# Sparse attention layer: the index keys' unit moved first, one root for both latents, index products between the query tiles

## The chip, the cores and the metric

The kernel runs on one core of a Trainium2 chip. The metric is the device time of one execution in microseconds, lower is better. A core has TensorE (PE, the matrix products; PEld is its weight load), VectorE (DVE), ScalarE (ACT), GpSimd (POOL) and SyncE (SP, which here only issues transfers). They run on their own and wait for one another through semaphores.

## The reference

The program is a decoder trunk of two layers over 512 tokens of width 1024. Each layer has a feed-forward part, a mixer, and another feed-forward part. The change is in the mixer of the second layer, a sparse attention with an index:

```python
q_lat = rmsnorm(h @ w_dq, q_norm_g)                        # 256 wide
q = (q_lat @ w_uq).reshape(bsz, s, DSA_HEADS, DSA_LATENT)  # 16 heads of 128
kv = rmsnorm(h @ w_dkv, kv_norm_g)                         # 128 wide
q_idx = (q_lat @ idx_w_q).reshape(bsz, s, IDX_HEADS, IDX_DIM)   # 16 heads of 64
k_idx = layernorm(h @ idx_w_k, idx_ln_g, idx_ln_b)         # 64 wide
w_idx = (h @ idx_w_w) * (IDX_HEADS ** -0.5 * IDX_DIM ** -0.5)
...
idx_logits = jnp.einsum('bqhd,bsd->bqhs', qib, k_idx)
score = jnp.einsum('bqhs,bqh->bqs', jax.nn.relu(idx_logits), wb)
score = jnp.where(causal, score, -jnp.inf)
_, sel = lax.top_k(score, topk)                            # the 128 best keys of a query
```

Each query then attends, with 16 heads, to its 128 selected keys alone, with a softmax and a relative-position bias.

## The kernel before

Activations lie transposed: a tile is 128 features by 512 tokens. Weights are streamed in units of 128 x 1024 numbers, in a ring of four slots. SP loads a unit into `w_raw`; ACT rounds it to `w_hi` (`produce_hi`, L471); DVE takes the rest, `w_lo` (`produce_lo`, L801); PE multiplies in three products per 128-row block (L1457 to L1459), which is why one unit of eight blocks is 24 matmuls. PE and each of the other engines follow their own instruction streams in the order in which the code was written; nothing is reordered.

The attention layer is `mix1`. Its head has four units. In the first two (`first_units`, L1476 to L1478) PE also forms the token norm: eight sums (L1549), and a spread of the root over the partitions (L1557). Units 0 and 1 give the query latent, unit 2 the key latent, unit 3 the index keys (64 rows) and index weights (16 rows). DVE scales each unit by the token norm (L1285, L1287, L1289). `latent_sums` (L1830) sums squares, `latent_rms` on DVE takes the root (some twelve tiny steps, L1274 and L813 to L818), `latent_spread` (L1836) spreads it. There are two such roots: one for the query latent, and a later one for the key latent and the index keys. The index keys are centred by a small product (L1857).

The body has 24 query tiles of six matmuls each (`q_tile`, L1881 to L1883): tiles 0 to 7 hold the index queries of two heads each, tiles 8 to 23 one head of attention queries each. ACT evicts them (L699). Then there are 48 index products r = 0 to 47 (L1902): three query blocks of 16 heads, each a product of 64 rows by 256, 384 or 512 keys. Even heads use partitions 0 to 63 of `index_q` and `index_k`, odd heads 64 to 127; the second copy of `index_k` is made by a transfer on POOL's queue (L452). ACT rectifies each product (L711), and DVE multiplies it by the head's weight and adds it up (L1343, L1346). From r = 16 on, DVE also runs the selection of the block before: MAX8 and MATCH_REPLACE8 (L1329, L1331), one round per product in block 2, one round per two products in block 3. The rings are four deep: PE's product r waits for the rectified product r - 4, and this one for DVE's sum r - 8:

```python
for r in range((TT - 1) * IH):
    ...
    if r >= 4:
        pe.wait_ge(d_relu, r - 3)
    pe.matmul(ps[:, r % 4, 0:w], ...).then_inc(d_ix, 1)
    if r % 3 == 2 and r // 3 < AH - 1:
        q_tile(KT + 1 + r // 3)
```

So before the change nine query tiles run first, and then three index products and one tile in turn. When DVE has done its last sum, the attention proper starts (L1364 on DVE, L1947 on PE).

Of the kernel before, what the change touches and what calls it, by code (L numbers as in the profile page):

```python
# [21 lines left out]
ALU = mybir.AluOpType  # L22
ACT = mybir.ActivationFunctionType
# [40 lines left out]
def build_program(nc, a, out):  # L64
    ctx = ExitStack()
    with ctx:
# [88 lines left out]
        index_k_centred = at("index_k_centred", [IDIM, TOK], 40)  # L155
# [13 lines left out]
        cmat = at("cmat", [IDIM, IDIM], 99)  # L169
# [57 lines left out]
        if "mix1" in UB:  # L227
            parts[UB["mix1"] + 3] = 3
# [48 lines left out]
        d_mul, d_hi, d_ql, d_kv, d_kn, d_dup, d_tr, d_trev = (sem("d_" + n) for n in ("mul", "hi", "ql", "kv", "index_k", "dup", "tr", "trev"))  # L277
# [5 lines left out]

        R0, X0, V_ORDER = 9, 17, (1, 2, 3, 0)
# [10 lines left out]
        def _(sp):  # L295
# [42 lines left out]
            def column_params():  # L338
# [5 lines left out]
                sp.dma_start(pcols[0:IDIM, 11:12], a["idx_ln_g"].rearrange("l h -> h l")).then_inc(cols_landed, 16)  # L344
                sp.dma_start(pcols[0:IDIM, 12:13], a["idx_ln_b"].rearrange("l h -> h l")).then_inc(cols_landed, 16)
# [57 lines left out]
        def _(pool):  # L403
# [33 lines left out]
            if "mix1" in STAGES:  # L437
# [13 lines left out]
                pool.wait_ge(d_kn, 2)  # L451
                pool.dma_start(index_k[IDIM:2 * IDIM, :], index_k[0:IDIM, :]).then_inc(d_dup, 16)  # L452
# [9 lines left out]
        def _(act):  # L462
# [77 lines left out]
            def mix0(nxt):  # L540

                n = UB["mix0"]
                act.wait_ge(cols_landed, 16 * 6)
# [130 lines left out]
            def mix1(nxt):  # L674
# [4 lines left out]
                for t in range(1, 4):  # L679

                    act.wait_ge(tile_out, 4 + T1 + t)
                    act.activation(sq[:, t - 1, :], q_latent_raw[:, t - 1, :] if t < 3 else kv_raw[:, :], ACT.Square).then_inc(d_raw, 1)
                    produce_hi(n + t + SLOTS)
# [3 lines left out]
                act.wait_ge(d_cen, 1)  # L687
# [15 lines left out]
                for t in range(KT):  # L703
                    q_out(t)
                q_out(KT)
                for r in range((TT - 1) * IH):
# [5 lines left out]
                    if r % 3 == 2 and r // 3 < AH - 1:  # L712
                        q_out(KT + 1 + r // 3)
# [1331 lines left out]
```

## Time and profile before

| | |
|---|---|
| median of three runs | 2184.98 us (2181.61 to 2185.51) |
| the profiled execution | 2183.87 us, its span 2182.1 us |
| PE busy | 2130.7 us, 98% of the span |
| PEld, DVE, ACT busy | 80%, 56%, 33% |
| POOL busy | 2% |
| mean granted TensorE clock | 0.992 |
| chain that ended last | PE 68%, DVE 8%, issue 2%, ACT 2% |
| DMA queues | q1 29.8% of the 16 engines' span |

The busy share is an average over very different stages: the feed-forward parts keep PE full, while the attention layer, about 1541 to 1770 us, has stretches in which DVE sets the pace. What a change there is worth has to be read there.

### The profile page before, as it was taken

The numbers are of one execution on the slowest core, as the hardware profiler recorded it, in microseconds if no ns is written. First come the engines' busy times: TensorE is split into PE (matmuls) and PEld (weight loads), VectorE is DVE, ScalarE is ACT, GpSimd is POOL, SyncE is SP. The second block draws the span as 40 slices with busy tenths as digits, with TensorE's granted clock in tenths as the row PEclk, the third lists the DMA queues.
The fourth block names the chain that finished last, engine by engine and source line by source line (L and its number), as shares of the span: only waits on it lengthen the run. The fifth ranks groups of instructions, "written<-read, shape, count | busy, mean of one in ns | idle before, by whom it ended". The sixth has DMA issues, their size and how long they took to land.

```text
span 2182.1 us, 27827 instructions
## 1 busy us (share of the span) xinstructions
PE 2130.7 (98%) x10065; PEld 1736.5 (80%) x10065; DVE 1225.0 (56%) x1948; ACT 729.9 (33%) x1013; POOL 51.8 (2%) x95
## 2 busy tenths in 40 slices
PE   8999999999999999999999999999997999999998
PEld 7888888788887778888888888888765678888887
DVE  6535446586658986445356544445578645435444
ACT  4222224334335542222224222223366643222223
POOL 0000000000000000000000000000002300000000
PEclk9999999999999999999999999999999999999999
DMA  6333424322243324454443333333300113333321
GB/s 171 96 99 96 110 83 105 91 65 59 68 127 90 83 69 115 106 116 106 112 105 106 102 97 96 96 96 87 87 23 1 40 49 97 96 97 96 97 84 61
DMA packets 357868, 195.14 MB, mean 89 GB/s; under 512 B 14747, under 2 KB 349734, under 8 KB 357782
## 3 DMA queue, kind: packets, MB, share of 16 engines
q1 hardware_dynamic: 355110, 184.21, 29.8%
q0 software_dynamic: 2672, 9.80, 2.8%
q8 instruction: 52, 0.85, 0.2%
q14 instruction: 34, 0.28, 0.0%
HBM read 191.07 MB, written 2.79 MB: 89 GB/s over the span
## 4 chain that ended last, share of the span: by engine, by line
PE 68%; DVE 8%; issue 2%; ACT 2%; DVEq 0%; ACTq 0%
PE ps L1457 19%; PE ps L1459 19%; PE ps L1458 19%; PE ps L1641 1%; PE ps L1947 1%; PE ps L1935 1%; DVE w_lo L801 1%; DVE index_scores L1346 1%; PE ps L1656 1%; PE ps L1657 1%; PE ps L1658 1%; PE ps L1476 1%; PE ps L1478 1%; PE ps L1477 1%; DVE index_scores L1331 1%
## 5 line engine op out<-in xcount | busy, mean ns | idle before, releaser
L471 ACT ACTIVATE w_hi<-w_raw 128x1024 fp32r<-128x1024 f32 x351 | 371.5, 1060 | 1055.1 <-PE ps L1459 974.4
L1457 PE MATMUL ps<-h_hi,w_hi 128*128 128x512 f32 x1632 | 637.6, 391 | 0.0
L1459 PE MATMUL ps<-h_hi,w_lo 128*128 128x512 f32 x1632 | 635.3, 389 | 0.0
L1458 PE MATMUL ps<-h_lo,w_hi 128*128 128x512 f32 x1632 | 635.2, 389 | 0.0
L801 DVE TENSOR_TENSOR w_lo<-w_raw,w_hi 128x1024 fp32r<-128x1024 f32 x351 | 428.8, 1222 | 288.3 <-ACT w_hi L471 288.1
L1457 PEld LDWEIGHTS ps<-h_hi,w_hi 128*128 128x128 f32 x1632 | 306.4, 188 | 65.3 <-issue 2.2
L1459 PEld LDWEIGHTS ps<-h_hi,w_lo 128*128 128x128 f32 x1632 | 306.4, 188 | 63.8
L1458 PEld LDWEIGHTS ps<-h_lo,w_hi 128*128 128x128 f32 x1632 | 306.5, 188 | 62.8
L1457 PE MATMUL ps<-act_hi,w_hi 128*128 128x512 f32 x704 | 274.1, 389 | 0.0
L1459 PE MATMUL ps<-act_hi,w_lo 128*128 128x512 f32 x704 | 274.0, 389 | 0.0
L1458 PE MATMUL ps<-act_lo,w_hi 128*128 128x512 f32 x704 | 274.0, 389 | 0.0
L907 DVE SCALAR_TENSOR_TENSOR x<-ps,x 128x512 f32 (+1 forms) x112 | 77.4, 691 | 276.2 <-PE ps L1459 275.2
L929 DVE TENSOR_TENSOR prod<-ps,rms_rows 128x512 f32<-128x512 f32 x88 | 60.8, 691 | 209.2 <-PE ps L1459 209.2
L1457 PEld LDWEIGHTS ps<-act_hi,w_hi 128*128 128x128 f32 x704 | 132.2, 188 | 27.5
L1459 PEld LDWEIGHTS ps<-act_hi,w_lo 128*128 128x128 f32 x704 | 132.2, 188 | 27.5
L1458 PEld LDWEIGHTS ps<-act_lo,w_hi 128*128 128x128 f32 x704 | 132.2, 188 | 27.2
L521 ACT ACTIVATE silu_gate<-silu_gate 128x512 f32<-128x512 f32 x88 | 55.6, 632 | 161.6 <-DVE silu_gate L926 161.5
L932 DVE TENSOR_TENSOR prod<-silu_gate,prod 128x512 f32<-128x512 f32 x88 | 60.9, 692 | 11.3 <-ACT silu_gate L521 1.4
L936 DVE TENSOR_TENSOR act_lo<-prod,act_hi 128x512 f32 (+1 forms) x88 | 60.9, 692 | 10.7 <-DVE act_hi L934 1.0
L926 DVE TENSOR_TENSOR silu_gate<-ps,rms_rows 128x512 f32<-128x512 f32 x88 | 60.1, 683 | 2.4 <-ACT rms_rows L502 2.4
L1947 PE MATMUL ps<-kvT,att_q 128*128 128x128 f32 (+3 forms) x128 | 49.4, 470 | 7.6 <-ACT sq L711 4.5
L1364 DVE CUSTOM_DVE_ANT_0 probs<-ps,bias_rows 128x128 f32<-128x128 f32 (+3 forms) x64 | 31.3, 490 | 29.3 <-PE ps L1948 28.5
(317 smaller groups left out, 2115.6 us busy)
## 6 DMA issues: line engine op xcount, KB each, us to landing
w_raw<-in_ffn_w_gate SPq DMA_DIRECT2D x88, 512.0 KB, 3.8
w_raw<-in_ffn_w_up SPq DMA_DIRECT2D x88, 512.0 KB, 3.8
w_raw<-in_ffn_w_down SPq DMA_DIRECT2D x64, 512.0 KB, 3.9
w_raw<-in_hy_w_in SPq DMA_DIRECT2D x44, 512.0 KB, 3.8
w_raw<-in_ffn_w_down SPq DMA_DIRECT2D x32, 384.0 KB, 3.4
w_raw<-in_hy_w_out SPq DMA_DIRECT2D x16, 512.0 KB, 4.1
acum_rows<-acum_scratch POOLq DMA_DIRECT2D x4, 1024.0 KB, 9.9
bias_rows<-line_scratch POOLq DMA_DIRECT2D x8, 512.0 KB, 6.9
```

The source lines that it names most:

```text
L471: act.activation(w_hi[:, s, :], w_raw[:, s, :], ACT.Copy).then_inc(hi_ready, 1)
L521: act.activation(silu_gate[:, j, :], silu_gate[:, j, :], ACT.Silu).then_inc(silu_done, 1)
L801: dve.tensor_tensor(w_lo[:, s, :], w_raw[:, s, :], w_hi[:, s, :].bitcast(F32), ALU.subtract).then_inc(lo_ready, 1)
L907: dve.scalar_tensor_tensor(out=xt, in0=ps[:, b:b + 1, :], scalar=scale, in1=xt, op0=ALU.mult, op1=ALU.add).then_inc(x_upd, 1)
L926: dve.tensor_tensor(silu_gate[:, j, :], ps[:, 2 * j, :], rms_rows[:, :], ALU.mult).then_inc(gate_scaled, 1)
L929: dve.tensor_tensor(prod[:, j, :], ps[:, 2 * j + 1, :], rms_rows[:, :], ALU.mult).then_inc(up_scaled, 1)
L932: dve.tensor_tensor(prod[:, j, :], silu_gate[:, j, :], prod[:, j, :], ALU.mult).then_inc(mul_done, 1)
L936: dve.tensor_tensor(act_lo[:, bass.ds(2 * i + j, 1), :], prod[:, j:j + 1, :], act_hi[:, bass.ds(2 * i + j, 1), :].bitcast(F32), ALU.subtra ...
L1457: pe.matmul(ps[:, bank, :], wh, rh[:, k, :], start=k == 0, stop=False)
L1458: pe.matmul(ps[:, bank, :], wh, rl[:, k, :], start=False, stop=False)
L1459: mm = pe.matmul(ps[:, bank, :], wl, rh[:, k, :], start=False, stop=k == nk - 1)
L1947: pe.matmul(ps[:, r % 2, 0:w], att_q[:, h, b * P:(b + 1) * P], kvT[:, 0:w], start=True, stop=False)
```

## The change

The units of the head are reordered: the index keys and weights first, then the two of the query latent, then the key latent. The centring product stands in the middle of unit 2; the index keys' sums and the transposes of the index weights stand behind unit 2. One root serves the index keys and the query latent together; it and its two spreads are placed inside unit 3. The key latent's sums, root and spread move among the first query tiles. The centring matrix is doubled in width, so that the index keys come out on all 128 partitions at once, and the transfer on POOL's queue is gone; two more small parameter transfers of 64 numbers each are issued at the start of the program. Of the body, tiles 2 to 9 are each followed by two index products (r = 0 to 15), tiles 10 to 22 by one each (r = 17 to 29), and behind tile 23 the other products (r = 30 to 47) follow one another with no tile between them. DVE's `w_lo` of four units moves in between the sums (`LOWS`).

```diff
--- before.py
+++ after.py
...
+        SCORE_BANKS, INTERLEAVED = (0, 3, 2, 1), 2 * KT
...
+                for r in (0, IDIM):
+                    sp.dma_start(pcols[r:r + IDIM, 11:12], a["idx_ln_g"].rearrange("l h -> h l")).then_inc(cols_landed, 16)
+                    sp.dma_start(pcols[r:r + IDIM, 12:13], a["idx_ln_b"].rearrange("l h -> h l")).then_inc(cols_landed, 16)
...
+                    s0 = slot(n)
+                    load(n, 0, [(s0[:, :, 0:IDIM], iw), (s0[:, :, IDIM:IDIM + IH], ww), (s0[:, :, IDIM + IH:P], dkv[:, :, IDIM + IH:P])])
                     for j in range(2):
-                        load(n + j, 0, [(slot(n + j), kp(a["dsa_w_dq"][0])[:, :, j * P:(j + 1) * P])])
-                    load(n + 2, 0, [(slot(n + 2), dkv)])
-                    s0 = slot(n + 3)
-                    load(n + 3, 0, [(s0[:, :, 0:IDIM], iw), (s0[:, :, IDIM:IDIM + IH], ww), (s0[:, :, IDIM + IH:P], dkv[:, :, IDIM + IH:P])])
+                        load(n + 1 + j, 0, [(slot(n + 1 + j), kp(a["dsa_w_dq"][0])[:, :, j * P:(j + 1) * P])])
+                    load(n + 3, 0, [(slot(n + 3), dkv)])
...
-                pool.wait_ge(d_kn, 2)
-                pool.dma_start(index_k[IDIM:2 * IDIM, :], index_k[0:IDIM, :]).then_inc(d_dup, 16)
...
+                produce_hi(n + 3 + SLOTS)
+                act.wait_ge(d_kvr, 1)
+                act.activation(sq[:, 2, :], kv_raw[:, :], ACT.Square).then_inc(d_raw, 1)
...
+                for t in range(KT + 2):
+                    q_out(t)
+                    if t >= 2:
+                        score_out(2 * t - 4)
+                        score_out(2 * t - 3)
+                for r in range(INTERLEAVED, (TT - 1) * IH):
+                    score_out(r)
+                    if r < INTERLEAVED + AH - 2:
+                        q_out(KT + 2 + r - INTERLEAVED)
...
+                def scaled(t, dst):
                     dve.wait_ge(unit_used, n + t + 1)
-                    b = 4 + (T1 + t) % 4
-                    if t < 3:
-                        dve.tensor_tensor(q_latent_raw[:, t, :] if t < 2 else kv_raw[:, :], ps[:, b, :], rms_rows[:, :], ALU.mult).then_inc(tile_out, 1)
-                    else:
-                        dve.tensor_tensor(index_k_raw[0:IDIM, :], ps[0:IDIM, b, :], rms_rows[0:IDIM, :], ALU.mult).then_inc(d_kx, 1)
...
+                latent_rms(1, 2, ((0, IDIM), (4, AQR)))
...
+                latent_rms(2, 2, ((0, AL),))
+
+                def latent_keys():
...
+                LOWS = {3: 2, 5: 3, 9: 4, 18: 5}
...
+                    if r == 1:
+                        latent_keys()
+                    if r in LOWS:
+                        produce_lo(n + LOWS[r] + SLOTS)
...
+                def blocks(t, ks):
+                    u = n + t
+                    if ks[0] == 0:
+                        pe.wait_ge(x_upd, XB["mix1"] - 3 + (T1 + t) % 4)
+                        pe.wait_ge(tile_out, T1 + t + 1)
+                        pe.wait_ge(lo_ready, u + 1)
+                    dst = ps[:, 4 + (T1 + t) % 4, :]
+                    for k in ks:
+                        wh, wl = w_hi[:, u % SLOTS, k * P:(k + 1) * P], w_lo[:, u % SLOTS, k * P:(k + 1) * P]
+                        pe.matmul(dst, wh, h_hi[:, k, :], start=k == 0, stop=False)
+                        pe.matmul(dst, wh, h_lo[:, k, :], start=False, stop=False)
+                        mm = pe.matmul(dst, wl, h_hi[:, k, :], start=False, stop=k == KT - 1)
+                        if k == KT - 1:
+                for t in range(2):
                     pe.wait_ge(x_upd, XB["mix1"] - 3 + (T1 + t) % 4)
                     pe.wait_ge(tile_out, T1 + t + 1)
-                    if t == 0:
-                        continue
-                    if t == 1:
-                        first_units(n, [4 + (T1 + u) % 4 for u in range(2)], "mix1")
-                        continue
-                    unit(n + t, 4 + (T1 + t) % 4, h_hi, h_lo, KT)
-                    if t == 2:
-                        pe.wait_ge(d_raw, 2)
-                        latent_sums(P, (0, 1), 2, 0).then_inc(d_ss, 1)
-                pe.wait_ge(d_rs, 1)
-                latent_spread(0, 0).then_inc(d_bc, 1)
-
+                first_units(n, [4 + (T1 + u) % 4 for u in range(2)], "mix1")
+                blocks(2, range(0, 4))
                 pe.wait_ge(a_const, 2)
                 pe.wait_ge(d_kx, 1)
-                pe.matmul(ps[0:IDIM, 1, :], cmat[:, :], index_k_raw[0:IDIM, :], start=True, stop=True).then_inc(d_cen, 1)
-
+                pe.matmul(ps[:, 1, :], cmat[:, :], index_k_raw[0:IDIM, :], start=True, stop=True).then_inc(d_cen, 1)
+                blocks(2, range(4, KT))
+                pe.wait_ge(d_sq, 1)
+                latent_sums(IDIM, (3,), 2, 0)
                 R = slice(IDIM, IDIM + IH)
-                pe.wait_ge(tile_out, T1 + 4 + 4)
+                pe.wait_ge(tile_out, T1 + 4 + 1)
                 for c in range(TT):
-                    mm = pe.transpose(ps[:, 2, c * IH:(c + 1) * IH], index_k_raw[R, c * P:(c + 1) * P], ident[R, R])
+                    mm = pe.transpose(ps[:, 0, c * IH:(c + 1) * IH], index_k_raw[R, c * P:(c + 1) * P], ident[R, R])
                 mm.then_inc(d_tr, 1)
-                pe.wait_ge(d_raw, 3)
+                blocks(3, range(0, 1))
+                pe.wait_ge(d_raw, 2)
+                latent_sums(P, (0, 1), 2, 4).then_inc(d_ss, 1)
+                blocks(3, range(1, 5))
+                pe.wait_ge(d_rs, 1)
+                pe.wait_ge(d_trev, 1)
+                latent_spread(0, 4).then_inc(d_bc, 1)
                 pe.wait_ge(rb_ready, XNORM["mix1"] + 1)
-                latent_sums(P, (2,), 3, 4)
-                pe.wait_ge(d_sq, 1)
-                latent_sums(IDIM, (3,), 3, 8).then_inc(d_ss, 1)
-                pe.wait_ge(d_ql, 2)
+                latent_spread(3, 0).then_inc(d_bc, 1)
+                blocks(3, range(5, KT))
...
-                for u in range(2):
-                    for j in range(4):
-                        q_tile(4 * u + j)
-                    if u == 0:
-                        pe.wait_ge(d_rs, 2)
-                        pe.wait_ge(d_kc, 1)
-                        latent_spread(1, 4)
-                        latent_spread(3, 8).then_inc(d_bc, 1)
-                q_tile(KT)
-                pe.wait_ge(tile_out, T1 + 4 + 4 + KT)
-                pe.wait_ge(d_dup, 16)
-                for r in range((TT - 1) * IH):
...
+                    if r < IH:
+                        pe.wait_ge(tile_out, T1 + 4 + 3 + h // 2 + 1)
+                    if r == 0:
+                        pe.wait_ge(d_kn, 2)
+                    if r == 2:
+                        pe.wait_ge(d_rs, 2)
+                    if r == 3:
+                        pe.wait_ge(d_kv, 1)
                     if r >= 4:
                         pe.wait_ge(d_relu, r - 3)
-                    pe.matmul(ps[:, r % 4, 0:w], index_q[R, h // 2, b * P:(b + 1) * P], index_k[R, 0:w], start=True, stop=True).then_inc(d_ix, 1)
-                    if r % 3 == 2 and r // 3 < AH - 1:
-                        q_tile(KT + 1 + r // 3)
+                    pe.matmul(ps[:, SCORE_BANKS[r % 4], 0:w], index_q[R, h // 2, b * P:(b + 1) * P], index_k[R, 0:w], start=True, stop=True).then_inc(d_ix, 1)
+                pe.wait_ge(d_ql, 2)
+                q_tile(0)
+                pe.wait_ge(d_raw, 3)
+                latent_sums(P, (2,), 2, 0).then_inc(d_ss, 1)
+                q_tile(1)
+                for t in range(2, KT + 2):
+                    if t == 3:
+                        pe.wait_ge(d_rs, 2)
+                        pe.wait_ge(d_kc, 1)
+                        latent_spread(1, 0).then_inc(d_bc, 1)
+                    q_tile(t)
+                    score(2 * t - 4)
+                    score(2 * t - 3)
+                for r in range(INTERLEAVED, (TT - 1) * IH):
+                    score(r)
+                    if r < INTERLEAVED + AH - 2:
+                        q_tile(KT + 2 + r - INTERLEAVED)
...
```

On PE, in the head, this is what stood behind the last blocks of unit 3: a spread, the centring product, the transposes of the index weights, and eight sums (of key latent and index keys), before the first query tile.

```order
L1459 MATMUL ps<-h_hi,w_lo 128x512
L1836 MATMUL ps<-ident,rs 128x128 x4
L1857 MATMUL ps<-index_k_raw,cmat 64x512
L1862 MATMUL ps<-ident,index_k_raw 128x16 x4
L1830 MATMUL ps<-ones,sq 128x128 x8
L1881 MATMUL ps<-q_latent_hi,w_hi 128x512
```

Now these stand apart. Between units 2 and 3, and inside unit 3, stand the sums of the index keys, the transposes, one block, and the sums of the query latent:

```order
L1845 MATMUL ps<-ones,sq 128x128 x4
L1882 MATMUL ps<-ident,index_k_raw 128x16 x4
L1863 MATMUL ps<-h_hi,w_hi 128x512
L1864 MATMUL ps<-h_lo,w_hi 128x512
L1865 MATMUL ps<-h_hi,w_lo 128x512
L1845 MATMUL ps<-ones,sq 128x128 x8
```

So the sums and transposes have moved from behind unit 3 to places ahead of it and inside it.

On PE, in the body, the old pattern, from product 0 to product 44, was three products, then the six matmuls of one tile:

```order
L1902 MATMUL ps<-index_k,index_q 128x256 x3
L1881 MATMUL ps<-q_latent_hi,w_hi 128x512
L1882 MATMUL ps<-q_latent_lo,w_hi 128x512
L1883 MATMUL ps<-q_latent_hi,w_lo 128x512
L1881 MATMUL ps<-q_latent_hi,w_hi 128x512
L1882 MATMUL ps<-q_latent_lo,w_hi 128x512
L1883 MATMUL ps<-q_latent_hi,w_lo 128x512
L1902 MATMUL ps<-index_k,index_q 128x256 x3
```

In the changed kernel, at products 14 and 15 (the last pair), 16, tile 10 and product 17:

```order
L1927 MATMUL ps<-index_k,index_q 128x256 x2
L1927 MATMUL ps<-index_k,index_q 128x384
L1908 MATMUL ps<-q_latent_hi,w_hi 128x512
L1909 MATMUL ps<-q_latent_lo,w_hi 128x512
L1910 MATMUL ps<-q_latent_hi,w_lo 128x512
L1908 MATMUL ps<-q_latent_hi,w_hi 128x512
L1909 MATMUL ps<-q_latent_lo,w_hi 128x512
L1910 MATMUL ps<-q_latent_hi,w_lo 128x512
L1927 MATMUL ps<-index_k,index_q 128x384
```

Products that stood in threes now stand alone between two tiles, thirteen times over (r = 17 to 29).

## Rows read from the trace of the kernel before

**Rows 1.** Busy time in stretches; behind POOL's come granted clock, DMA share, GB/s.

```profile
1553.41:1575.66 22.25, 19.92 (x98) 15.91 (x96) 11.83 (x25) 7.88 (x12) 0.00 (x0) 0.88 0.32 95
1575.66:1592.32 16.66, 16.66 (x71) 13.60 (x71) 5.31 (x18) 6.38 (x10) 0.56 (x1) 0.85 0.15 40
...
1607.07:1629.48 22.41, 22.41 (x85) 11.95 (x85) 21.79 (x67) 14.16 (x28) 0.00 (x0) 1.00 0.00 1
1629.48:1650.91 21.43, 13.81 (x44) 6.68 (x44) 20.08 (x43) 9.64 (x17) 0.00 (x0) 0.88 0.00 0
1651.11:1656.42 5.31, 4.97 (x13) 3.24 (x14) 4.26 (x21) 4.37 (x13) 0.72 (x2) 0.55 0.01 2
```

**Rows 2.** Waits of DVE, 1607 to 1651 us: total, times, longest.

```profile
DVE index_scores L1346 <- DVE index_scores L1346: 0.5, 1, 0.5
```

**Rows 3.** Timeline of DVE: start, us, engine, line, operation.

```profile
1626.59 0.61 DVE L1346 SCALAR_TENSOR_TENSOR index_scores<-sq,index_w_tok,index_scores 128x384 f32<-128x384 f32 x1
...
1627.97 0.61 DVE L1346 SCALAR_TENSOR_TENSOR index_scores<-sq,index_w_tok,index_scores 128x384 f32<-128x384 f32 x1
...
1650.91 0.28 DVE L1319 TENSOR_TENSOR index_scores<-index_scores,causal_neg 128x128 f32<-128x128 f32 x1
1651.11 0.28 DVE L1364 CUSTOM_DVE_ANT_0 probs<-ps,bias_rows 128x128 f32<-128x128 f32 x1
```

**Rows 4.** Timeline of PE in the head of the layer.

```profile
1553.41 0.48 PE L1457 MATMUL ps<-h_hi,w_hi 128*128 128x512 f32 x1
...
1559.20 2.05 PE L1830 MATMUL ps<-ones,sq 128*128 128x128 f32 x16
1561.01 0.47 PE L1457 MATMUL ps<-h_hi,w_hi 128*128 128x512 f32 x1
...
1566.58 1.05 PE L1836 MATMUL ps<-ident,rs 128*128 128x128 f32 x8
1569.89 1.30 PE L1857 MATMUL ps<-index_k_raw,cmat 64*64 64x512 f32 x2 [2.26 <-DVE index_k_raw L1287]
...
1571.65 4.08 PE L1830 MATMUL ps<-ones,sq 128*128 128x128 f32 x16
1575.66 0.79 PE L1881 MATMUL ps<-q_latent_hi,w_hi 128*128 128x512 f32 x1
```

**Rows 5.** Timeline of PE, index products (L1902) and query tiles (from L1881).

```profile
1597.60 1.13 PE L1902 MATMUL ps<-index_k,index_q 64*128 64x256 f32 x6
1598.66 0.50 PE L1881 MATMUL ps<-q_latent_hi,w_hi 128*128 128x512 f32 x1
...
1608.37 1.55 PE L1902 MATMUL ps<-index_k,index_q 64*128 64x384 f32 x6
1609.86 0.50 PE L1881 MATMUL ps<-q_latent_hi,w_hi 128*128 128x512 f32 x1
...
1611.44 1.55 PE L1902 MATMUL ps<-index_k,index_q 64*128 64x384 f32 x6
...
1634.40 1.25 PE L1902 MATMUL ps<-index_k,index_q 64*128 64x512 f32 x4
1636.20 1.12 PE L1902 MATMUL ps<-index_k,index_q 64*128 64x512 f32 x2 [0.54 <-ACT sq L711]
1637.25 0.50 PE L1881 MATMUL ps<-q_latent_hi,w_hi 128*128 128x512 f32 x1
```

**Rows 6.** Timeline of DVE, query operands.

```profile
1570.49 1.41 DVE L1293 SCALAR_TENSOR_TENSOR sq<-q_latent_raw,gains,ps 128x512 f32<-128x512 f32 x2
1571.93 1.35 DVE L1297 TENSOR_TENSOR q_latent_lo<-sq,q_latent_hi 128x512 fp32r<-128x512 f32 x2
```

**Rows 7.** Timeline of ACT, one burst of rectified products.

```profile
1609.32 1.26 ACT L711 ACTIVATE sq<-ps 128x384 f32<-128x384 f32 x3 [0.24 <-PE ps L1902]
```

**Rows 8.** Timeline at the start of the program, ACT and PE.

```profile
31.88 1.06 ACT L471 ACTIVATE w_hi<-w_raw 128x1024 fp32r<-128x1024 f32 x1 [7.66 <-DMA w_raw<-in_ffn_w_gate]
...
37.36 0.39 PE L1457 MATMUL ps<-h_hi,w_hi 128*128 128x512 f32 x1
```

More of the change, by code:

```diff
@@ L276, in build_program @@
         d_raw, d_kx, d_cen, d_kc, d_sq, d_ss, d_rs, d_bc = (sem("d_" + n) for n in ("raw", "index_k_raw", "cen", "index_k_centred", "sq", "ss", "rs", "bc"))
-        d_mul, d_hi, d_ql, d_kv, d_kn, d_dup, d_tr, d_trev = (sem("d_" + n) for n in ("mul", "hi", "ql", "kv", "index_k", "dup", "tr", "trev"))
+        d_mul, d_hi, d_ql, d_kvr, d_kv, d_kn, d_tr, d_trev = (sem("d_" + n) for n in ("mul", "hi", "ql", "kv_raw", "kv", "index_k", "tr", "trev"))
         d_tile, d_ix, d_relu, d_acc = sem("d_tile"), sem("d_ix"), sem("d_relu"), sem("d_acc")
@@ L678, in mix1 @@
                 rms_out("mix1")
[L679 to L683, printed above, removed]
+                produce_hi(n + 1 + SLOTS)
+                act.wait_ge(tile_out, T1 + 4 + 2)
+                act.activation(sq[:, 0, :], q_latent_raw[:, 0, :], ACT.Square).then_inc(d_raw, 1)
+                act.wait_ge(d_cen, 1)
+                act.activation(sq[0:IDIM, 3, :], ps[0:IDIM, 1, :], ACT.Square).then_inc(d_sq, 1)
+                act.activation(index_k_centred[:, :], ps[:, 1, :], ACT.Copy).then_inc(d_kc, 1)
+                act.wait_ge(tile_out, T1 + 4 + 3)
+                act.activation(sq[:, 1, :], q_latent_raw[:, 1, :], ACT.Square).then_inc(d_raw, 1)
+                produce_hi(n + 2 + SLOTS)
+                act.wait_ge(d_tr, 1)
+                act.activation(index_w_tok[:, :, :], ps[:, 0, 0:TT * IH].rearrange("p (c h) -> p c h", c=TT), ACT.Copy).then_inc(d_trev, 1)
                 for d in range(2):
@@ L702, in q_out, with score_out @@
                         produce_hi(n + 4 + t // 4 + SLOTS)
-                for t in range(KT):
-                    q_out(t)
-                q_out(KT)
-                for r in range((TT - 1) * IH):
+                def score_out(r):
                     w = P * (r // IH + 2)
@@ L710, in mix1 @@
                         act.wait_ge(d_acc, r - 3)
-                    act.activation(sq[:, r % 4, 0:w], ps[:, r % 4, 0:w], ACT.Relu).then_inc(d_relu, 1)
-                    if r % 3 == 2 and r // 3 < AH - 1:
-                        q_out(KT + 1 + r // 3)
+                    act.activation(sq[:, r % 4, 0:w], ps[:, SCORE_BANKS[r % 4], 0:w], ACT.Relu).then_inc(d_relu, 1)
+                for t in range(KT + 2):
[7 more added lines that the diff above has]
+                        q_out(KT + 2 + r - INTERLEAVED)
                 NR = TT * AH
@@ L1838, in latent_spread @@
                     return mm
-                for t in range(4):
+                def blocks(t, ks):
[11 more added lines that the diff above has]
+                        if k == KT - 1:
+                            mm.then_inc(unit_used, 1)
@@ L1875, in q_tile @@
                         pe.wait_ge(lo_ready, n + 4 + u + 1)
-                    pe.wait_ge(tile_out, T1 + 4 + t + 1)
+                    if t == 3:
+                        pe.wait_ge(d_kvr, 1)
+                    else:
+                        pe.wait_ge(tile_out, T1 + 4 + (t + 1 if t < 3 else t))
                     dst = ps[:, 4 + (T1 + t) % 4, :]
```

67 lines of the change are left out of this document (31 added, 36 removed).

## The prediction

> **What bounds the kernel now.** I took the windows of the attention layer first, since the engine that sets the pace changes from stage to stage [rows 1]. In the head and the first tiles PE is the full engine, apart from one idle spot, and the granted clock there is 0.88 and 0.85. From 1607.07 us it turns: DVE is busy 21.79 us of 22.41 and then 20.08 of 21.43. The waits of DVE over these 44 us show one of 0.5 us on its own sum, by way of ACT, and none on PE inside the stretch [rows 2]. So from product r = 16 on, DVE's chain of sum and selection decides, one product every 1.38 us in block 2, and it ends at 1650.91; at 1651.11 DVE goes straight on to the attention [rows 3]. PE, which is full until about 1641, only has to stay ahead. The end of this DVE chain is the number that the change must move; what follows it is not edited.
>
> The timeline of PE in the head shows what can be saved there [rows 4]: 2.26 us idle before the centring product (DVE first has to scale unit 3), and then a stretch at half clock: sixteen records of sums take 4.01 us (1571.65 to 1575.66) that took 1.81 us earlier (1559.20 to 1561.01). Since 1 - 0.88 of 22.25 us and 1 - 0.85 of 16.66 us were lost at half rate, the low stretch was some 10 us long (5.3 + 5.0): the clock fell to 1.2 GHz after the idle spot and came back with PE working.
>
> **The head, new.** Until 1553.41 nothing differs. From there, work at full clock: units 2 and 3 at 5.57 us each (1561.01 to 1566.58 [rows 4]), 11.14; they are now cut into five pieces, three restarts more at 0.1, an estimate from the first matmul's 0.47 against 0.39 in the middle, 0.3; the centring product alone, 1.05 (the product of 64 rows by 512 that stood alone, 1636.20 to 1637.25 [rows 5]) and the transposes, together 1.6 (they took 1.76 with the clock falling, 1569.89 to 1571.65 [rows 4]); twelve products of sums at 1.81/8, 2.7; eight of spreads, priced alike, 1.8. Sum 17.5, so 1570.9. Waits: after the first spread, DVE and ACT need 2.8 us for the query operands (1570.49 to 1573.28 [rows 6]), and PE has the second spread and nine matmuls, 0.9 + 2.1 = 3.0, as cover. The root is covered by twelve matmuls, 2.8 us; nothing shows it to be longer by more than tenths. I take 0.1 for both, and 0 to 1 as bounds. Tile 0 starts at 1571.0 instead of 1575.66: **4.7 us earlier**.
>
> **The body, new.** Tile 0 takes 1.4 (1.58 from 1609.86 to 1611.44 with the change of mode around it [rows 5]; six steps of 5.57/24 without it). Then PE waits for the squares of the key latent: ACT first makes a `w_hi` that only unit 3's end releases, 1.06 [rows 8], then the square, some 0.6, together with signals 1.9 against tile 0's 1.4: 0.5, bounds 0 to 1. Sums 0.9, tiles 1 and 2 with their changes 2.9: product 0 at 1576.7. What does a pair cost? Three products of 256 took 1.06, of 384 1.49 [rows 5]. The rows at 512 show two in 1.25 (1634.40) and one alone in 1.12 (1636.20): an even and an odd head run beside each other, and the third waits. So a burst of three is two turns; it grows by 0.43 per 128 columns, a turn by 0.21. A lone product is one turn: 1.05 at 512, hence 0.84 at 384, 0.63 at 256, and a pair costs the same as one. Then: pair 0.63, spread 0.9, giving 1578.2; seven times tile and pair at 1.58 + 0.63, 15.5, giving 1593.7; product 16 joins the last pair, 0.6. Tile 10 starts at 1594.3. Product 16 starts at 1593.7 and reaches DVE some 1.4 later, at 1595.1, against 1607.07 before: 12.0 us earlier.
>
> But now each tile is followed by one lone product: 1.58 + 0.84 = **2.42 us per product, where DVE wants one every 1.38**. PE has become the bound of this stretch. Thirteen such turns are 31.5 us; with tile 23 product 30 starts at 1627.4. It reaches DVE 1.45 us later: 0.95 to ACT's start (1608.37 [rows 5] to 1609.32 [rows 7]) and about 0.5 for ACT: 1628.8. From there DVE is the bound again. Before, it went from product 30 (1626.59) to the end (1650.91) in 24.3 us [rows 3]; less the 0.5 us wait [rows 2], in which ACT had other work between the products, 23.9. The chain ends at 1652.7 instead of 1650.91: **1.8 us later**. All that the head and the first 16 products gain is spent between product 16 and product 30: fourteen steps that took DVE 19.5 us (1607.07 to 1626.59) now take PE 33.7, so 14.2 lost against 12.0 and 0.5 gained.
>
> Bounds of the lone product: below, a third of a burst, 1.49/3 = 0.50, 4.4 us less over thirteen; above, the 1.05 of a 512 product, 2.7 us more. I take 0.84, since the lone row at 512 is the same operation in the same place. The Trainium skill speaks of this in "TensorEngine Tiling (Array Packing)", Tiling Modes, Key Properties: a change of tiling mode drains TensorE. By that rule the change pays for 22 entries into 64-row products instead of 16; the trace agrees with a cost, 1.58 against 1.39 for a tile, and it is in my 1.58. Six more at 0.19 are 1.1 us; were mode changes free, the sum would be 4.2 lower.
>
> **Edits costed at nothing.** The duplicate's transfer on POOL: PE did not wait for it, and POOL has nothing else then. DVE's `w_lo` amid the sums, 1.22 each: a turn of tile and pair leaves DVE 2.21 - 1.1. The three narrow loads of the index unit come three units earlier, at a ring lead of six units. Two more parameter transfers at the start, behind which SP's weight loads queue: the fifth unit came late there, ACT waited 7.66 us and rounded it at 31.88, DVE needs 1.2 more, and PE, in order, takes it at 37.36 [rows 8]: 3.2 us of cover for some 1.1 us of issue.
>
> **Sum.** 2183.87 + 1.8 = 2185.7 us by the profiled execution's own time, which lies 1.1 below the median of 2184.98; by the median it is 2186.8. I say 2186.0. About 4.4 us (0.2%) is what a measurement of this kernel can tell from no change.
>
> **The rivals.** *A, faster: DVE stays the bound from product 16 on.* It would start its chain at 1593.7 + 1.4 = 1595.1 instead of 1607.07 and end 12.4 us earlier: 2171.5 us. It needs a PE turn of at most 1.38; the tile alone is 1.58 [rows 5]. Chance 0.04. *B, cheap lone products*, at 0.50: 1.8 - 4.4 = -2.6, 2181.3 us. For it: the second pass may overlap a tile's first. Against: 1637.25. Chance 0.10, a third of it beyond 4.4 with shorter waits. *C, slower: the clock.* From 1629 on PE has 18 products and no tile, half idle for 20 us, and the clock may be low where the attention starts. Before, a low stretch of some 10 us began near 1645.6, so that 4.8 us of it lay in the attention's first 5.3 us (clock 0.55 [rows 1]). If all of it lies there, 5.4 us more at half rate with PE 94% busy are at most 2.7 us: +4.5, 2188.4 us. For it: the idle gap before the attention remains. Against: it was there before too, and it may as well fall away (-2.4). It decides where the low stretch begins behind 1650. The skill's page "TensorE: Matmul & The Clock Gate", Part 1, says that activity releases the throttle and idleness brings it back; by it the thin stretch itself could fall too. At half clock a turn of a pair 512 wide would be twice 1.05, 2.1 us, still under the 2.7 that DVE takes for two products in block 3 (21.43 us for 16). Chance 0.13. *D, slower: the start.* If the 128 extra four-byte elements hold the fifth unit up by more than 3.2 us, each us beyond is lost. Chance 0.03.
>
> **How the numbers follow.** Forecast 0.70, A 0.04, B 0.10, C 0.13, D 0.03. Beyond 0.2% faster: A, a third of B, and measurement, 0.09. Slower: most of C and D and the upper bound of the lone product, 0.16. Within: 0.75. Range: B's 2181 below, C's and the upper bound's 2190 above; the forecast's own is 2183 to 2189.
>
> **What the profile would show.** No idle spot and clock 1.00 until tile 0 near 1571; product 16 near 1594; from there PE without idle time and DVE idle about 1 us before each sum, released by ACT; product 30 near 1627; DVE's chain full after it, ending near 1652.7, two us later than before. I am wrong if the PE turn is under 2.2 us, if DVE's chain ends before 1649, or if the attention after it runs at another clock than before.

## The result and the profile after

The changed kernel takes 2188.20 us (median of 12 runs, 2186.57 to 2188.98), the kernel before 2184.67 (12 runs, 2181.22 to 2185.51). The medians differ by 3.5 us (0.16%); the ratio taken over all of these runs is 1.0019, with a 95% interval of 1.0012 to 1.0026: slower, and just inside the 0.2% that I had set as the limit of "no change", with part of the interval outside it. Predicted were 2186.0 us (2181 to 2190) and "within 0.2%" with a chance of 0.75. Two of the runs of the kernel before beside the experiments below (2336.7 and 2673.76 us, mean granted clock 0.87 and 0.75) were slow from a low clock and are left out of every ratio.

PE is busy 2135.2 us (98% of a span of 2185.4), 4.5 more than before. The windows of the changed kernel's attention layer (columns as in [rows 1]) are the head, the pairs, the lone products, the thin stretch, and the start of the attention:

```profile
1554.41:1572.28 17.87, 17.87 (x98) 13.85 (x96) 9.22 (x23) 6.20 (x10) 0.00 (x0) 1.00 0.20 60
1572.28:1594.88 22.60, 22.47 (x109) 14.93 (x109) 14.57 (x34) 13.62 (x28) 0.00 (x0) 1.00 0.24 71
1594.88:1628.69 33.81, 33.81 (x114) 18.69 (x111) 21.74 (x58) 17.97 (x33) 0.00 (x0) 1.00 0.06 16
1628.69:1654.73 26.04, 18.73 (x45) 7.64 (x44) 23.37 (x53) 11.53 (x20) 0.00 (x0) 0.74 0.00 0
1654.93:1660.24 5.31, 4.96 (x18) 3.17 (x19) 4.62 (x22) 4.39 (x14) 1.14 (x4) 0.68 0.00 2
```

The head is full and at full clock, as was hoped. But from product 16 to product 30 PE is busy for every bit of 33.81 us, and DVE only for 21.74 of them. The view of DVE's waits, 1594 to 1655 us, names what it waited for:

```profile
DVE index_scores L1357 <- ACT sq L713: 13.6, 14, 1.5
```

Fourteen waits of about 1 us, where [rows 2] had one of 0.5. ACT is named because it signals last. The timelines of PE in the head, then around products 14 to 18 and at product 30, show who was late:

```profile
1553.62 1.05 PE L1572 MATMUL ps<-ident,rs 128*128 128x128 f32 x8
1557.35 1.12 PE L1875 MATMUL ps<-index_k_raw,cmat 64*128 64x512 f32 x2
1561.37 1.16 PE L1845 MATMUL ps<-ones,sq 64*128 64x128 f32 x8
...
1568.23 2.05 PE L1851 MATMUL ps<-ident,rs 128*128 128x128 f32 x16
1572.28 0.50 PE L1908 MATMUL ps<-q_latent_hi,w_hi 128*128 128x512 f32 x1
...
1577.93 0.70 PE L1927 MATMUL ps<-index_k,index_q 64*128 64x256 f32 x4
...
1583.25 0.70 PE L1927 MATMUL ps<-index_k,index_q 64*128 64x256 f32 x4
...
1585.47 0.70 PE L1927 MATMUL ps<-index_k,index_q 64*128 64x256 f32 x4
...
1594.35 1.34 PE L1927 MATMUL ps<-index_k,index_q 64*128 64x256 f32 x6
1595.62 0.50 PE L1908 MATMUL ps<-q_latent_hi,w_hi 128*128 128x512 f32 x1
...
1597.20 0.91 PE L1927 MATMUL ps<-index_k,index_q 64*128 64x384 f32 x2
1598.05 0.50 PE L1908 MATMUL ps<-q_latent_hi,w_hi 128*128 128x512 f32 x1
...
1599.63 0.59 PE L1927 MATMUL ps<-index_k,index_q 64*128 64x384 f32 x1
...
1628.69 1.77 PE L1927 MATMUL ps<-index_k,index_q 64*128 64x384 f32 x8
```

Each index product leaves two records. A turn of tile and pair is 1585.47 - 1583.25 = 2.22 us; a turn of tile and lone product is 1599.63 - 1597.20 = 2.42, of which the product takes 0.84 (1597.20 to 1598.05). DVE at products 16 and 30, and at the end of its chain:

```profile
1596.48 0.42 DVE L1354 TENSOR_SCALAR index_scores<-sq,index_w_tok 128x384 f32<-128x384 f32 x1
...
1630.76 0.62 DVE L1357 SCALAR_TENSOR_TENSOR index_scores<-sq,index_w_tok,index_scores 128x384 f32<-128x384 f32 x1 [1.53 <-ACT sq L713]
...
1654.73 0.28 DVE L1330 TENSOR_TENSOR index_scores<-index_scores,causal_neg 128x128 f32<-128x128 f32 x1
1654.93 0.28 DVE L1379 CUSTOM_DVE_ANT_0 probs<-ps,bias_rows 128x128 f32<-128x128 f32 x1
```

The chain starts 10.6 us earlier than in [rows 1] (1607.07) and ends 3.8 us later than in [rows 3].

**The start of the program has to be taken out first.** The spread of the token norm's root, the last step that both kernels have alike, starts at 1553.62 here and at 1552.60 before: 1.02 us of the 3.8 are older than the layer. They come from the first matmuls of the program. The timeline of PE there, of the kernel before and of the changed one:

```profile
11.00 0.39 PE L1506 MATMUL ps<-h_lo,w_hi 128*128 128x512 f32 x1
```

```profile
11.33 0.63 PE L1521 MATMUL ps<-h_lo,w_hi 128*128 128x512 f32 x1
```

In the profile before, a step (from one matmul to the next) takes 0.23 us from the first weight unit on; in this one it takes 0.43 us until about 14.5 us. A step of 0.43 is what the same matmul takes where the granted clock reads 0.50 (1.2 GHz; 1576.25 to 1576.68 in the profile before). Here, though, the granted clock reads 1.00 in both profiles. The window of the changed kernel:

```profile
9.00:16.00 7.00, 6.46 (x26) 5.13 (x25) 6.00 (x8) 3.92 (x7) 0.00 (x0) 1.00 1.12 298
```

So that PE was at half clock here is inferred from the steps alone, and not shown by the clock's record; I call it the slow start. Whether the edit does this is what the first and the last experiment ask. With the start taken out, the layer's chain ends 1654.73 - 1650.91 - 1.02 = 2.8 us later than before.

### The profile page after: what moved, and what is told of

It reads as the page before. It is cut to its first block, busy times and chain, and to the rows that moved or that the text cites. A ratio compares the mean times of both kernels' runs of the same rounds, so it can differ in the third digit from the quotient of the medians.

```text
span 2185.4 us, 27857 instructions
## 1 busy us (share of the span) xinstructions
PE 2135.2 (98%) x10065; PEld 1732.6 (79%) x10065; DVE 1226.7 (56%) x1948; ACT 731.3 (33%) x1013; POOL 51.2 (2%) x94
## 4 chain that ended last, share of the span: by engine, by line
PE 69%; DVE 7%; issue 2%; ACT 2%; DVEq 0%; ACTq 0%
PE ps L1472 19%; PE ps L1474 19%; PE ps L1473 19%; PE ps L1656 1%; PE ps L1987 1%; PE ps L1975 1%; PE ps L1927 1%; DVE w_lo L810 1%; PE ps L1908 1%; PE ps L1671 1%; PE ps L1672 1%; PE ps L1673 1%; PE ps L1491 1%; PE ps L1492 1%; PE ps L1493 1%
## 5 line engine op out<-in xcount | busy, mean ns | idle before, releaser
L1472 PE MATMUL ps<-h_hi,w_hi 128*128 128x512 f32 x1616 | 630.9, 390 | 0.0
L1474 PE MATMUL ps<-h_hi,w_lo 128*128 128x512 f32 x1616 | 628.8, 389 | 0.0
L1473 PE MATMUL ps<-h_lo,w_hi 128*128 128x512 f32 x1616 | 628.8, 389 | 0.0
L457 POOL TENSOR_SCALAR probs<-probs,stat 128x128 f32<-128x128 f32 (+3 forms) x64 | 34.3, 548 | 596.8 <-DVE stat L1391 596.7
```

The costliest lines, as they stand in the source:

```text
L1472: pe.matmul(ps[:, bank, :], wh, rh[:, k, :], start=k == 0, stop=False)
L1473: pe.matmul(ps[:, bank, :], wh, rl[:, k, :], start=False, stop=False)
L1474: mm = pe.matmul(ps[:, bank, :], wl, rh[:, k, :], start=False, stop=k == nk - 1)
```

## The experiments

Runs 1 to 4 shared one chip (the kernel before: 2185.34 us there), runs 5 to 8 another (2185.01). "Start" is the place of that spread, against 1552.60.

**1. Two added parameter transfers alone**, in the kernel before:

```diff
-                sp.dma_start(pcols[0:IDIM, 11:12], a["idx_ln_g"]...).then_inc(cols_landed, 16)
-                sp.dma_start(pcols[0:IDIM, 12:13], a["idx_ln_b"]...).then_inc(cols_landed, 16)
+                for r in (0, IDIM):
+                    sp.dma_start(pcols[r:r + IDIM, 11:12], a["idx_ln_g"]...).then_inc(cols_landed, 16)
+                    sp.dma_start(pcols[r:r + IDIM, 12:13], a["idx_ln_b"]...).then_inc(cols_landed, 16)
...
-                act.wait_ge(cols_landed, 16 * 6)
+                act.wait_ge(cols_landed, 16 * 8)
...
```

> The kernel before, with nothing but the two extra parameter transfers at the start of the program. Theory (the layer alone makes the change slower, by some 2.4 us; the 1.0 us by which the changed kernel's profile already lags at 50 us is the clock at the program's start, which differs from run to run): same time as before, within 0.5 us. Rival (the two transfers cost part of the 3.5 us): slower by about 1 us, with the fifth weight unit rounded 0.6 us later and PE late from there on.

Measured: 2184.3 us, ratio 0.9996 (0.9987 to 1.0005). The transfers cost nothing that can be measured. Its profile brought something else, in PE's timeline of the head, and in DVE's at product 16:

```profile
1572.26 1.07 PE L1858 MATMUL ps<-index_k_raw,cmat 64*64 64x512 f32 x2 [2.26 <-DVE index_k_raw L1288]
1573.26 0.42 PE L1863 MATMUL ps<-ident,index_k_raw 16*128 16x16 f32 x4
```

```profile
1605.80 0.42 DVE L1344 TENSOR_SCALAR index_scores<-sq,index_w_tok 128x384 f32<-128x384 f32 x1
```

The same idle 2.26 us as in [rows 4], and yet the centring product takes 1.07 and not 1.30: here the clock did not fall behind the idle spot. DVE's product 16 comes 50.8 us behind the spread (1554.96 to 1605.80), against 54.5 before. So 3.6 us of the profile before are a half-clock stretch (1570.54 to 1580.78, granted clock 0.50) that another execution of the same work doesn't have; they are still there at the end of DVE's chain (94.7 us behind the spread here, 98.3 before). One thing is odd in this profile: its granted clock reads 0.95 over most of the program (0.946 in the mean), though its steps take the same 0.23 us as elsewhere at 1.00. I have no explanation for it.

**2. Two products behind every tile** of the second part, instead of one:

```diff
-                    if r < INTERLEAVED + AH - 2:
-                        q_tile(KT + 2 + r - INTERLEAVED)
+                    if r % 2 and r < INTERLEAVED + 2 * (AH - 2):
+                        q_tile(KT + 2 + (r - INTERLEAVED) // 2)
...
```

ACT's evictions follow the same order, here and in runs 3 and 4.

> The changed kernel, but from product 16 on a query tile stands behind every second product instead of behind every product (tiles 10 to 23 behind products 17, 19 ... 43). Theory (a lone product costs 0.84, a pair costs the same, because the two run beside each other): PE's turn is 2.42 us for two products, DVE wants 2.77 for two, so DVE is the bound from product 16 on; its chain of 43.4 us starts near 1595.3 and ends near 1638.7 plus the start's offset: about 2172.5 us, 12 us faster than before and 15 faster than the changed kernel. Rival (PE's cost is per product, 0.5 to 0.84 each, and tiles are the load whatever their order): a turn of 2.6 to 3.3 us for two, the same tiles and the same work in all: 2176 to 2186 us. Rival (the attention or ACT gives it back): DVE's chain ends 12 us earlier but the time falls by less than 9.

Measured: 2173.78 us (2173.3 to 2175.39), ratio 0.9949 (0.9935 to 0.9962), 11.6 us under the kernel before on the same chip, and 14.4 under the changed kernel's median, which was taken beside other runs of the kernel before (0.7 us lower). PE's timeline, one window, and DVE's waits from 1594 to 1655 us:

```profile
1597.49 0.92 PE L1927 MATMUL ps<-index_k,index_q 64*128 64x384 f32 x4
...
1599.92 0.92 PE L1927 MATMUL ps<-index_k,index_q 64*128 64x384 f32 x4
```

```profile
1594.63:1614.51 19.88, 19.88 (x85) 11.19 (x85) 18.18 (x53) 14.20 (x28) 0.00 (x0) 1.00 0.10 28
```

```profile
DVE probs L1379 <- PE ps L1988: 2.4, 5, 0.7
DVE index_scores L1357 <- ACT sq L713: 1.5, 2, 1.1
```

A tile with two products takes 2.43 us, a tile with one took 2.42. The second product is free. Per product that is 1.22 us, less than DVE's 1.38, and DVE's waits on its sums fall from 13.6 us to 1.5. This is the one edit on which the loss hung. The expected 2172.5 left out one term: DVE's chain from product 16 on took 44.6 us, not 43.4, since one `w_lo` of 1.22 us stands in it (see run 3).

**3. The new head with the old body** (nine tiles, then three products and a tile in turn, as before the change; the first `w_lo` of the body goes ahead of it):

```diff
-                for t in range(2, KT + 2):
+                for t in range(2, KT + 1):
...
-                    score(2 * t - 4)
-                    score(2 * t - 3)
-                for r in range(INTERLEAVED, (TT - 1) * IH):
+                for r in range((TT - 1) * IH):
                     score(r)
-                    if r < INTERLEAVED + AH - 2:
-                        q_tile(KT + 2 + r - INTERLEAVED)
+                    if r % 3 == 2 and r // 3 < AH - 1:
+                        q_tile(KT + 1 + r // 3)
```

> The changed kernel's head with the old order of the body: tiles 0 to 8 first, then three products and a tile in turn. Theory (the head is worth what the trace of the change shows, and only the lone products spoil it): tile 0 at 1571 instead of 1575.7, no stretch at half clock before the products, product 0 near 1586 instead of 1592.3; DVE the bound from product 16 on as before, everything 6.5 us earlier: about 2178.2 us. Rival (the head's gain is not real, it only moves the low clock to a later place): 2182 to 2185 us, with the granted clock falling somewhere between 1586 and 1640.

Measured: 2180.0 us (2179.17 to 2181.51), ratio 0.9976 (0.9967 to 0.9985): the head alone is worth 5.3 us against its neighbours on the chip. DVE, at product 16:

```profile
1602.98 0.41 DVE L1352 TENSOR_SCALAR index_scores<-sq,index_w_tok 128x384 f32<-128x384 f32 x1
```

That is 48.5 us behind the spread (1554.50), 6.0 less than in the profile before; by run 1, 3.6 of it are the half-clock stretch, and the other 2.4 are close to the idle spot's 2.26. At the end of DVE's chain (1647.62, 93.1 behind the spread) only 5.2 of the 6.0 are left, which fits the median. The 0.8 went to DVE: a `w_lo`, which before the change stood ahead of the sums (the last at 1592.64), now stands in the chain behind product 18, while the old wait of 0.5 us is gone:

```profile
1606.40 1.22 DVE L807 TENSOR_TENSOR w_lo<-w_raw,w_hi 128x1024 fp32r<-128x1024 f32 x1
```

The median was 1.8 us above the 2178.2 that I expected: the gain is 5.3 where I had 6.5, and the kernel before itself took 0.7 more in these runs. The rival had the granted clock fall between 1586 and 1640; it read 1.00 up to 1640 us. This profile alone has steps of 0.43 us at the start of the output projection (1760.53 to 1763.65), but it is the slowest of the eleven executions, and the median doesn't rest on it.

**4. Two tiles, then two products:** the tiles at the pace of the changed kernel, but no lone product.

```diff
-                    if r < INTERLEAVED + AH - 2:
-                        q_tile(KT + 2 + r - INTERLEAVED)
+                    if r % 2 and r < INTERLEAVED + AH - 2:
+                        for t in range(2):
+                            q_tile(KT + 1 + r - INTERLEAVED + t)
...
```

> The changed kernel with the same ratio of tiles to products from product 16 to 30, but in pairs: two tiles, then two products. Theory (two products side by side cost as one): 3.81 us for two products and two tiles instead of 4.84; product 30 starts 7.2 us earlier than in the changed kernel, and the time is 7 us less than the changed kernel's, about 2181.0 us. Rival (no sharing; only changes of mode cost): 14 lone products cost the same in pairs, seven changes of mode at 0.19 are saved: 1.3 us less than the changed kernel, 2186.9 us.

Measured: 2180.25 us (2179.21 to 2181.69), ratio 0.998 (0.9971 to 0.9989). PE's timeline, and DVE's waits on its sums:

```profile
1598.75 0.92 PE L1928 MATMUL ps<-index_k,index_q 64*128 64x384 f32 x4
...
1602.56 0.92 PE L1928 MATMUL ps<-index_k,index_q 64*128 64x384 f32 x4
...
1621.59 1.77 PE L1928 MATMUL ps<-index_k,index_q 64*128 64x384 f32 x8
```

```profile
DVE index_scores L1358 <- ACT sq L713: 6.9, 7, 1.5
```

With the same fourteen products and as many tiles, product 30 starts at 1621.59 instead of 1628.69. A turn is 3.81 for two products, 1.90 each: PE is still the bound, but half as much. What the changed kernel lost was not the tiles' place but the half of each turn that a lone product leaves empty, and the second change of mode (a turn of two tiles and a pair is 3.81, where two turns of tile and lone product are 4.84; no run takes the two parts of this 1.03 apart).

**5. Both products of a pair on the same 64 rows**, in the changed kernel: the heads of the first query block in the order 0, 2, 1, 3 of every four.

```diff
+                    if r < IH:
+                        h = 4 * (h // 4) + (0, 2, 1, 3)[h % 4]
...
```

> The changed kernel, with one edit: in the first query block the heads are taken in the order 0, 2, 1, 3 of every four, so that both products of a pair use the same 64 rows of PE; the sums and their weights follow the same order, so the work is the same. Theory (two products of different 64 rows run beside each other, and a pair costs one turn): the second product of each pair now costs a turn of its own, some 0.43 us at 256 columns by 1.05 for 512; seven turns lie ahead of product 16, which then starts 3.0 to 3.5 us later against the changed kernel's 1594.9, and since PE is the bound to product 30, the end moves by the same: about 3.3 us slower than the changed kernel (1.0015 of it). Rival (products do not run beside each other, and a pair is cheap because the second hides behind the first's pipeline, whatever its rows): the turn of tile and pair stays 2.2 us and the time stays that of the changed kernel.

Measured: 2190.18 us, ratio 1.0024 (1.0015 to 1.0033), 2.8 us above the changed kernel on that chip (2187.42, run 7). PE's timeline:

```profile
1584.46 1.13 PE L1930 MATMUL ps<-index_k,index_q 64*128 64x256 f32 x4
...
1587.10 1.13 PE L1930 MATMUL ps<-index_k,index_q 64*128 64x256 f32 x4
```

The pair takes 1.13 by its records instead of 0.70, the turn 2.64 instead of 2.22. Seven turns at 0.42 are 2.9 us; tile 10 starts at 1598.71 instead of 1595.62, 3.1 later, 0.4 of it from the start of the program; the end of DVE's chain lies 2.7 us further behind the spread. The loss is a little under the 3.0 to 3.5 forecast, since product 16, on the other rows, now runs beside product 15. Whether products run beside each other is thus a matter of their rows, and the rival falls. The Trainium skill says so in "TensorEngine Tiling (Array Packing)", Tiling Modes, Key Properties: different tiles of the array can run their matmuls in parallel; the traces agree (a pair in 0.70 us on different rows, in 1.13 on the same).

**6. ACT's rounding of tile 23's weight unit moved** from ahead of product 30 to behind product 35:

```diff
-                    if t % 4 == 3:
+                    if t % 4 == 3 and t < KT + AH - 1:
...
+                    if r == 35:
+                        produce_hi(n + 9 + SLOTS)
```

> The changed kernel, with one edit on ACT: the rounding of the ring unit that tile 23 releases (1.06 us of ACT) stands behind the rectified product 35 instead of ahead of product 30. Theory: product 30 reached DVE 2.06 us after PE started it, where 1.45 was forecast, because this rounding stood ahead of it; with the edit the lag is again 1.4 to 1.5 us, DVE's chain behind product 30 starts and ends about 0.6 us earlier, and the kernel is 0.5 to 0.7 us faster (0.9997 of the changed one, in the trace and hardly in the median). Rival (the lag comes from the signals of a full PE): lag and end stay.

Measured: 2186.58 us, ratio 1.0011 (1.0002 to 1.002), where run 7 has 1.0013. ACT's timeline at product 30, of the changed kernel and then of this one, with DVE's sum behind it:

```profile
1628.80 0.60 ACT L703 ACTIVATE att_q<-ps 128x512 f32<-128x512 f32 x1 [1.09 <-PE ps L1910]
1629.29 1.05 ACT L471 ACTIVATE w_hi<-w_raw 128x1024 fp32r<-128x1024 f32 x1
1630.24 2.33 ACT L713 ACTIVATE sq<-ps 128x384 f32<-128x384 f32 x5
```

```profile
1627.93 0.60 ACT L703 ACTIVATE att_q<-ps 128x512 f32<-128x512 f32 x1 [1.09 <-PE ps L1912]
1628.77 2.43 ACT L713 ACTIVATE sq<-ps 128x384 f32<-128x384 f32 x5 [0.24 <-PE ps L1929]
...
1629.29 0.62 DVE L1359 SCALAR_TENSOR_TENSOR index_scores<-sq,index_w_tok,index_scores 128x384 f32<-128x384 f32 x1 [0.94 <-ACT sq L713]
```

Product 30 (1627.82 on PE) reaches DVE after 1.47 us instead of 2.07, and DVE's chain ends 100.5 us behind the spread instead of 101.1: the mechanism holds. But the 0.6 us are lost again within the layer. The attention's first 5.31 us ran at a granted clock of 0.50 instead of 0.68:

```profile
1653.46:1658.77 5.31, 4.96 (x13) 3.33 (x14) 4.27 (x21) 4.36 (x13) 0.72 (x2) 0.50 0.01 2
```

and the output projection starts 214.3 us behind the spread (1767.03), where the changed kernel has 214.2 (1767.79). In this execution, then, the layer gained nothing, and the median, 0.8 us under run 7's, is too coarse to tell.

**7 and 8. Both kernels again, unedited.**

> The changed kernel, unedited, a second time, for another profile and time beside the same runs of the kernel before. Theory: PE's stretch at half clock at the start of the program and the place of the half-clock stretch near the attention are what differs from one execution to another; the chain of DVE again starts near 1596.5 and ends near 1652.9 if the start is again at half clock, one us earlier if not, with product 30 reaching DVE 2.06 us after PE starts it. Ratio to the kernel before again 1.001 to 1.003. Rival (the place of the half-clock stretches belongs to the kernel): both traces agree to a tenth of a us also there.

> The kernel before, unedited, a second time, for another profile. The five profiles of kernels with the two added parameter transfers all have PE at half clock until about 15 us after the start, and the one of the kernel before has not. Theory (chance of an execution, worth 1 us): half clock at the start may show here too. Rival (the added transfers keep PE's clock low at the start): full clock from 10.7 us again.

Measured: the changed kernel 2187.42 us, ratio 1.0013 (1.0004 to 1.0023); its second trace agrees with the first within 0.1 us (the spread 1553.61, DVE's chain ending at 1654.70, the output projection at 1767.82), and in the half-clock stretches too. My theory for run 7, that these differ, was not borne out by it. The kernel before, once more: 2184.73 us, span 2182.9. PE's timeline at the start and at the spread, the end of DVE's chain, and the window of the attention's first 5.31 us:

```profile
11.93 0.63 PE L1507 MATMUL ps<-h_hi,w_lo 128*128 128x512 f32 x1
...
1553.92 1.05 PE L1557 MATMUL ps<-ident,rs 128*128 128x128 f32 x8
```

```profile
1652.26 0.28 DVE L1319 TENSOR_TENSOR index_scores<-index_scores,causal_neg 128x128 f32<-128x128 f32 x1
```

```profile
1652.46:1657.77 5.31, 4.97 (x18) 3.14 (x19) 4.73 (x22) 4.54 (x14) 0.73 (x2) 0.68 0.01 2
```

Now the kernel before has the slow start too, and the spread comes at 1553.92. And run 6, which has the added transfers, has it not (its spread at 1552.74):

```profile
11.16 0.40 PE L1523 MATMUL ps<-h_lo,w_hi 128*128 128x512 f32 x1
```

So the 1.02 us are neither the edit's nor the transfers': over the ten profiles the spread lies between 1552.60 and 1554.96, in either kernel. Less its start, the second trace of the kernel before ends its chain at 1652.26 - 1.32 = 1650.94, as the first did (1650.91). The chain of 2.8 us more stands against both.

## Why the prediction was right

It named the right bound, the right price and the right place, and the mechanism held. The size came out larger than forecast: 3.5 us between the medians, where the sum had 1.8. That "within 0.2%" held was a near thing: the ratio is 1.0019, with an interval that reaches over 1.002; in run 7 it is 1.0013. Times of the changed kernel are given less 1.02.

- **Head.** Tile 0 at 1571.0 was forecast, 1571.26 came. The waits that I took at 0.1 and 0.5 were next to nothing: PE idled 0.13 us in the window of the pairs; product 0 came at 1576.91 (forecast 1576.7), so the pieces of work themselves were a little longer than I had them. Run 1 corrects a reading, though: I put the whole 4.7 down to the head's order, and of the 11.6 us that DVE's product 16 came earlier, 3.6 are a half-clock stretch that not every execution of the kernel before has.
- **Pairs.** 2.21 forecast, 2.22 measured; product 16 on PE near 1593.7 forecast, 1594.88 - 1.02 = 1593.86 measured. That a pair costs one turn because the heads use different rows is shown by run 5.
- **Lone products.** 0.84 and 2.42 forecast, 0.84 and 2.42 measured; product 30 on PE at 1627.4 forecast, 1627.67 measured. Run 2 shows that the second half of each turn was free, run 4 that without lone products 7 us of the 14 come back. Rival B, cheap lone products, fell. Rival A, DVE as the bound from product 16 on, needed the PE turn under 1.38 per product; run 2 makes that so and lands 2.3 us above the 2171.5 that I had worked out for it.
- **Product 30 to DVE: the mis-sized term.** I took 1.45 us from a burst of the kernel before and it took 2.07, since ACT rounds tile 23's weight unit just there (run 6). I had counted one such rounding, beside tile 0, but not this one. It is +0.6.
- **DVE's chain from product 30.** 23.9 forecast, 1654.73 - 1630.76 = 23.97 measured.
- **The attention.** I costed it at nothing, and named the clock as rival C, with the low stretch falling wholly into the attention. It moved the other way, forward into the thin stretch (granted clock 0.74 there, against 0.88 in [rows 1]), and C's price was not paid: the attention's first 5.31 us ran at 0.68 against 0.55, and the layer's output projection starts 112.9 us behind the attention's first step (1767.79), where it was 113.3 (1764.40): 0.4 gained. By my own third sign ("another clock than before") I would be wrong here; but the second trace of the kernel before has 0.68 and the same 0.4, so it is no effect of the change. Over all ten profiles this distance lies between 112.7 and 113.8 us: zero was a size that one execution may miss by about 1 us. At half clock PE had room in the thin stretch, as worked out: DVE's chain kept its pace.
- **The sum.** +1.8 forecast. Measured: 0.3 from small sums up to product 30, 0.6 from ACT, 0.1 in DVE's chain, and the 1.8 give 2.8 at the chain's end; -0.4 in the attention; +1.0 from the start. That is 3.4 between the two profiled executions (2183.87 and 2187.3). It is partly luck that the medians differ by as much (3.5): the start's 1.0 and the attention's 0.4 belong to these executions, and in run 7 the medians are only 2.4 apart. What the change does to the layer up to the end of DVE's chain is 2.8, against either trace of the kernel before; against run 1, which has no half-clock stretch in the head, it would be 6.4.
- **Costed at nothing**, and right for this kernel: the added transfers (run 1), POOL's transfer, the narrow loads and DVE's `w_lo`, beside which PE shows no wait. The `w_lo` is free only as long as DVE waits for PE anyway; where DVE is the bound, it costs about 1 us (runs 2 and 3).

What is left open: I have not shown why the clock stays up behind the idle spot in one execution and not in another, nor how often it does. Of the 12 timed runs of the kernel before, three lie at 2181.2 to 2181.6 us and nine at 2183.6 to 2185.5, a distance near those 3.6 us; that the three are executions without the half-clock stretch is a guess. The 52 runs of the kernel before beside the experiments fit it: five lie at 2181.3 to 2181.6 us with a mean granted clock of 0.995 or 0.996, the others at 2183.4 to 2186.4 with 0.991 to 0.994, and 10.24 us at half clock are 0.002 of the span. But none of the five was profiled.

## What to carry to other kernels

When small matmuls are threaded between large ones, price a turn, not a matmul: two products on different halves of the rows cost what one does (2.43 us against 2.42 here), so an odd one out throws half its place away. Then compare the turn per item with what the consumer takes per item (1.22 or 2.42 against 1.38): a thread that is finer than the consumer needs starves it, and a gain of 10.6 us ahead of it was gone fourteen products later. The order with two products behind each tile is the one to keep: 2173.78 us (five runs), 0.5% under the kernel before. And what is hidden behind one bound is not free once the bound moves: the same 1.22 us of DVE cost nothing in the changed kernel and about 1 us in run 2.

## What the runs showed of the hardware

- PE's first steps took 0.43 us in eight of ten profiles, and 0.23 in the first one of the kernel before and in run 6, while the granted clock read 0.98 or more in all ten (10 to 20 us); the layer's start moved by up to 2.4 us over the ten. The Trainium skill says in "TensorE: Matmul & The Clock Gate", Part 1, that the slow part at a kernel's start differs from run to run; the steps of these traces agree.
- Behind the same 2.26 us of idle PE the clock fell in two executions of the kernel before and stayed up in run 1, worth 3.6 us at product 16. In the first profile it then stayed at 0.50 from 1570.54 to 1580.78 us, with PE busy all that time, and came back to 1.00.
- The clock fell to 1.2 GHz also in the thin stretch of the changed kernel (PE busy 18.73 of 26.04 us, mean granted clock 0.74). Of PE's timeline there, two rows, four records each, and the window in which the clock fell:

```profile
1635.09 1.99 PE L1927 MATMUL ps<-index_k,index_q 64*128 64x512 f32 x4 [0.46 <-ACT sq L713]
1637.74 2.30 PE L1927 MATMUL ps<-index_k,index_q 64*128 64x512 f32 x4 [0.66 <-ACT sq L713]
```

```profile
1638.00:1640.00 2.00, 2.00 (x4) 0.33 (x3) 1.86 (x5) 0.81 (x2) 0.00 (x0) 0.82 0.00 0
```

The granted clock is 1.00 in the two us before this window and 0.50 in the two behind it, so it fell near 1639.3, inside the second row, which is already the longer one. From product 30 on PE had waited no longer than 0.7 us at a time until then.
